# A two-layer decoder kernel: forget and query projections turned to features on partitions, chunk sums by scans, values turned after their product, another order of the last tiles

## What is computed

```python
forget = lb + (1 - lb) * sigmoid(f)          # lb: one lower bound per feature
q, k, log_f = silu(q), 1 - forget, log(forget)
b = cumsum(log_f)                            # inside each chunk of 32 tokens
q_dec = q * exp(b)
k_inv = k * exp(-b)
k_tail = k * exp(b_last - b)
scores = tril(q_dec @ k_inv.T)
o = scores @ v + q_dec @ state
state = state * exp(b_last) + k_tail.T @ v
```

## Time and profile before

| | |
|---|---|
| median of 3 runs | 1162.54 us (1162.41 to 1162.78) |
| profiled execution | 1162.58 us, span 1160.5 us |
| TensorE matmul busy | 1133.5 us (98%) |
| VectorE busy | 895.1 us (77%) |
| ScalarE busy | 752.8 us (65%) |
| GpSimd busy | 131.5 us (11%) |
| granted TensorE clock, mean | 0.998 |

### The profile page before, as it was taken

The page is one execution under the profiler, slowest core; times in us unless marked ns, Lnnn a source line. Parts: engine busy times, 40 slices in busy tenths (PEclk is TensorE's granted clock), DMA queues, the critical chain, the costliest instruction groups (busy, mean ns, idle before and its releaser), DMA issues.

```text
span 1160.5 us, 17159 instructions
## 1 busy us (share of the span) xinstructions
PE 1133.5 (98%) x5862; PEld 900.0 (78%) x5862; DVE 895.1 (77%) x1233; ACT 752.8 (65%) x960; POOL 131.5 (11%) x91
## 2 busy tenths in 40 slices
PE   9999999999999999999999999999999999999996
PEld 7778777776888888888788875776888888888775
DVE  6542468637999999999885359836999999999886
ACT  7563122445887888778665449645878888788665
POOL 0000000001221212211000000001212122121000
PEclk9999999999999999999999999999999999999999
DMA  9662222523999999999761220322899999999731
GB/s 368 250 234 73 73 74 73 177 96 122 336 377 380 379 388 371 382 374 380 277 276 68 95 73 2 146 105 96 323 361 378 391 374 384 376 372 390 267 137 73
DMA packets 50596, 286.30 MB, mean 247 GB/s; under 512 B 9321, under 2 KB 9597, under 8 KB 21358
## 3 DMA queue, kind: packets, MB, share of 16 engines
q1 hardware_dynamic: 37086, 250.93, 56.5%
q0 software_dynamic: 13456, 34.65, 8.1%
HBM read 271.38 MB, written 30.41 MB: 260 GB/s over the span
## 4 chain that ended last, share of the span: by engine, by line
PE 86%; DVE 6%; ACT 3%; DMA 3%; issue 1%; SPq 0%; ACTq 0%; POOLq 0%; DVEq 0%
PE psum L568 80%; PE psum L974 2%; DVE arena L2689 2%; ACT whi L1416 2%; DMA arena<-vscr,cur 1%; DVE arena L2702 1%; PE psum L1015 1%; DMA arena<-yscr 1%; DVE wlo L1987 1%; DMA raw<-w_dense_dram 1%; PE psum L885 1%; ACT ahi L1416 1%; DVE wlo L1991 0%; ACT arena L1416 0%; DVE h L2522 0%
## 5 line engine op out<-in xcount | busy, mean ns | idle before, releaser
L1987 DVE TENSOR_TENSOR wlo<-raw,whi 128x2048 fp32r<-128x2048 f32 x200 | 456.1, 2289 | 70.6 <-ACT whi L1416 57.4
L568 PE MATMUL psum<-whi,ahi 128*128 128x512 f32 (+1 forms) x1184 | 468.0, 397 | 4.8 <-ACT ahi L1416 4.4
L568 PE MATMUL psum<-wlo,ahi 128*128 128x512 f32 (+1 forms) x1184 | 456.6, 387 | 0.9 <-DVE wlo L1991 0.9
L568 PE MATMUL psum<-whi,alo 128*128 128x512 f32 (+1 forms) x1184 | 451.9, 387 | 0.0
L1416 ACT ACTIVATE whi<-raw 128x2048 fp32r<-128x2048 f32 x200 | 382.8, 1916 | 44.5 <-PE psum L568 44.5
L568 PEld LDWEIGHTS psum<-whi,ahi 128*128 128x128 f32 x1184 | 222.5, 188 | 53.8 <-issue 6.8
L568 PEld LDWEIGHTS psum<-whi,alo 128*128 128x128 f32 x1184 | 222.3, 188 | 46.3
L568 PEld LDWEIGHTS psum<-wlo,ahi 128*128 128x128 f32 x1184 | 222.6, 188 | 42.8 <-DVE wlo L1991 1.3
L1416 ACT ACTIVATE arena<-psum 128x512 f32<-128x512 f32 (+3 forms) x150 | 83.2, 564 | 114.6 <-PE psum L568 90.6
L1416 ACT ACTIVATE ahi<-psum 128x512 fp32r<-128x512 f32 x146 | 82.0, 592 | 86.6 <-PE psum L974 39.3
L2797 POOL DMA_INDIRECT arena<-vscr,cur x32 | 69.5, 2171 | 386.0 <-DVE cur L2408 370.8
(11 more groups left out here) (221 smaller groups left out, 893.8 us busy)
## 6 DMA issues: line engine op xcount, KB each, us to landing
raw<-w_moe_dram SPq DMA_DIRECT2D x192, 1024.0 KB, 8.8
raw<-w_dense_dram SPq DMA_DIRECT2D x34, 1024.0 KB, 9.0
yscr<-arena POOLq DMA_DIRECT2D x2, 4096.0 KB, 23.1
arena<-yscr SPq DMA_DIRECT2D x6, 1024.0 KB, 7.3
vscr<-arena POOLq DMA_DIRECT2D x8, 512.0 KB, 2.9
h<-x_dram SPq DMA_DIRECT2D x4, 512.0 KB, 7.8
arena<-w_proj_dram POOLq DMA_DIRECT2D x2, 1024.0 KB, 7.7
arena<-yscr SPq DMA_DIRECT2D x4, 512.0 KB, 4.5
```

The lines of the kernel that those rows point to most:

```text
L568: return nc.tensor.matmul(o, l, r, start=start, stop=stop, **kw)
L1987: tt(wlo[:, b % SPL, :], raw[:, b % RAW, :], halves(whi[:, b % SPL, :]), ALU.subtract).then_inc(lo_ready, 1)
```

## The change

- The blocks' order is v, f, q, g. v keeps the form "act"; f and q are made with weights stationary, so that bank hh is head hh with time along columns.
- The lower bound is one number per partition; VectorE scales the sigmoid in one pass (multiply and add by per-partition numbers). `lower` goes.
- The chunk sum is VectorE's `tensor_tensor_scan` per head: state = keep * state + log f, with keep 0 at each chunk's first token; then b_last - b by a subtraction. `cum` goes, with its constant matrices; the exponentials read SBUF.
- Inverse keys and decayed queries come out in the form that the score products need; `kq_T` goes. The tail keys now have to be turned: `tail_T`, four transposes behind each of the first four tiles of g, copied out by ScalarE.
- The values of the attention are made like the keys (24 products of 512 columns), multiplied by the tokens' norm (VectorE), turned by four transposes behind aq1's first tile, and get their bias as they leave PSUM.
- The last `dense` goes through its tiles in the order `ENDS`; ScalarE and VectorE finish token block 2 ahead of the last gate.

The diff, cut to what the prediction speaks of:

```diff
-BLK = {"f": 0, "q": 1, "v": 2, "g": 3, "C": 4, "H": 5, "B": 6, "out0": 7, "ple0": 9,
+BLK = {"v": 0, "f": 1, "q": 2, "g": 3, "C": 4, "H": 5, "B": 6, "out0": 7, "ple0": 9,
...
+ENDS = [(0, 0), (0, 1), (1, 0), (0, 2), (1, 1), (1, 2), (0, 3), (1, 3)]
...
-        READ = {1: (g_sig, 0), 2: (g_silu, 0), 3: (g_v, 0), 8: (s_add, 0), 10: (M[0]["gt"], 0),
+        READ = {1: (g_v, 0), 2: (g_sig, 0), 3: (g_silu, 0), 8: (s_add, 0), 10: (M[0]["gt"], 0),
...
-                    sp.wait_ge(M[1]["gt"], 8 + tb)
+                    sp.wait_ge(M[1]["sg"], TB + tb)
...
-                    pe.wait_ge(*((t_z, 5) if q == 0 else (t_v, q)))
+                    pe.wait_ge(*((t_z, 5), (t_v, 1), (t_z, 3), (t_v, 2))[q])
...
-            def lower(i, q):
...
-                for hh in range(HEADS):
-                    last = mm(PS[4][:, hh * P:(hh + 1) * P], area(AR_ONE32, P), diag[:, hh, :],
-                              True, True)
-                last.then_inc(g_cum, 1)
...
-            dense(BLK["f"], "act", before=wait_first, mid=later_T, after=lower, order=TILES[1:],
+            dense(BLK["v"], "act", before=wait_first, mid=later_T, order=TILES[1:],
...
-            def cum(tb):
-                pe.wait_ge(g_log, tb + 2)
+            def tail_T(tb):
...
-                mm(PS[4][:, :], hc("triI"), F[:, tb, :], True, True)
-                mm(PS[5][:, :], hc("triS"), F[:, tb, :], True, True)
+                    pe.wait_ge(g_ktail, HEADS)
...
-                    at = (tb * HEADS + hh) * CPB
-                    last = mm(PS[6][:, at:at + CPB], F[:, tb, hh * P:(hh + 1) * P], hc("ind"),
-                              True, True)
-                last.then_inc(g_cum, 1)
-            def kq_T(tb):
...
-                for bank, at in ((7, AR_F), (6, AR_Q)):
-                    for hh in range(HEADS):
-                        last = nc.tensor.transpose(PS[bank][:, hh * P:(hh + 1) * P],
-                                                   area(at, TB, 512)[:, tb, hh * P:(hh + 1) * P],
-                                                   ident)
-                    last.then_inc(g_kqT, 1)
-            dense(BLK["q"], "act", after=lambda i, q: cum(q) if i == 1 else None)
-            dense(BLK["v"], "act", after=lambda i, q: kq_T(q) if i == 1 else None)
+                    last = nc.tensor.transpose(PS[4 + tb][:, hh * P:(hh + 1) * P],
+                                               area(AR_F, HEADS, SEQ)[:, hh, tb * P:(tb + 1) * P],
+                                               ident)
+                last.then_inc(g_kqT, 1)
+            dense(BLK["f"], "w")
+            dense(BLK["q"], "w")
...
+                pe.wait_ge(g_KT, tb + 1)
...
-                    pe.wait_ge(g_KT, TB)
-                    pe.wait_ge(g_QT, TB)
+                    pe.wait_ge(g_kinv, HEADS)
+                    pe.wait_ge(g_qdec, HEADS)
+                cols = slice(tb * P, (tb + 1) * P)
...
-                    last = mm(PS[4 + tb][:, hh * P:(hh + 1) * P], KT_[:, tb, hh * P:(hh + 1) * P],
-                              QT_[:, tb, hh * P:(hh + 1) * P], True, True)
+                    last = mm(PS[4 + tb][:, hh * P:(hh + 1) * P], KT_[:, hh, cols],
+                              QT_[:, hh, cols], True, True)
...
-            dense(BLK["g"], "act", after=lambda i, q: scores(q) if i == 1 else None)
+            dense(BLK["g"], "act", after=lambda i, q: scores(q) if i == 1 else tail_T(q))
...
-                          QT_[:, tb, hh * P + c * CHUNK:hh * P + (c + 1) * CHUNK],
+                          QT_[:, hh, n * CHUNK:(n + 1) * CHUNK],
...
-                    pe.wait_ge(g_ktail, TB)
+                    pe.wait_ge(g_KT, TB)
...
                 else:
-                    dense(k + 1, "act")
+                    dense(k + 1, "act", order=ENDS)
...
-            for q in range(4):
+            for q in range(2):
...
-                            t_ = slice(tb * P, (tb + 1) * P)
-                            mm(o, ahi[:, kt, t_], whi[:, s, w], kt == 0, False)
-                            mm(o, ahi[:, kt, t_], wlo[:, s, w], False, False)
-                            last = mm(o, alo[:, kt, t_], whi[:, s, w], False, kt == KT - 1)
...
+                o = PS[q][:, :]
+                for kt in range(KT):
+                    w = slice(kt * 256 + q * P, kt * 256 + (q + 1) * P)
+                    mm(o, whi[:, s, w], ahi[:, kt, :], kt == 0, False)
+                    mm(o, whi[:, s, w], alo[:, kt, :], False, False)
+                    last = mm(o, wlo[:, s, w], ahi[:, kt, :], False, kt == KT - 1)
+                if q == 0:
+                    last.then_inc(d_done, 3)
+                else:
+                    last.then_inc(w_used, 1)
+            def value_T():
+                pe.wait_ge(t_v, 1)
+                pe.wait_ge(t_z, 4)
+                for t in range(TB):
+                    last = nc.tensor.transpose(PS[3][:, t * P:(t + 1) * P],
+                                               area(AR_VT1, SEQ)[:, t * P:(t + 1) * P], ident)
+                last.then_inc(t_pT, 1)
...
+                if i == 0 and q == 0:
+                    value_T()
                 if i == 0 and 0 < q < 3:
...
             nc.scalar.activation(e3, e3, ACT.Exp).then_inc(g_log, 1)
...
+            B = area(AR_G, HEADS, SEQ)
             splits(4)
-            for tb in range(TB):
-                group_done(act, BLK["f"], tb)
-                nc.scalar.activation(F[:, tb, :], PS[tb][:, :], ACT.Sigmoid).then_inc(g_sig, 1)
-            splits(5)
-            for tb in range(TB):
-                act.wait_ge(g_k, tb + 3)
-                nc.scalar.activation(F[:, tb, :], F[:, tb, :], ACT.Ln).then_inc(g_log, 1)
-            dec = area(AR_DEC, 64)
-            def query(tb):
-                group_done(act, BLK["q"], tb)
-                nc.scalar.activation(Q[:, tb, :], PS[tb][:, :], ACT.Silu).then_inc(g_silu, 1)
-            for tb in range(TB):
...
-                nc.scalar.activation(E[:, tb, :], PS[4][:, :], ACT.Exp).then_inc(g_eb, 1)
-                nc.scalar.activation(et, PS[4][:, :], ACT.Exp, scale=-1.0).then_inc(g_enb, 1)
...
-                nc.scalar.activation(yt, PS[5][:, :], ACT.Exp).then_inc(g_esf, 1)
...
-            splits(8)
             act.wait_ge(n_t, 2 * TB + 1)
...
                 copy(V[:, tb, :], PS[tb][:, :]).then_inc(g_v, 1)
-                act.wait_ge(g_kqT, 2 * tb + 2)
-                copy(Q[:, tb, :], PS[6][:, :]).then_inc(g_QT, 1)
+            splits(6)
+            for hh in range(HEADS):
+                group_done(act, BLK["f"], hh)
+                nc.scalar.activation(F[:, hh, :], PS[hh][:, :], ACT.Sigmoid).then_inc(g_sig, 1)
+            for hh in range(HEADS):
+                act.wait_ge(g_k, hh + 2)
+                nc.scalar.activation(F[:, hh, :], F[:, hh, :], ACT.Ln).then_inc(g_log, 1)
+            splits(7)
+            for hh in range(HEADS):
+                act.wait_ge(g_cum, hh + 1)
+                nc.scalar.activation(F[:, hh, :], F[:, hh, :], ACT.Exp).then_inc(g_esf, 1)
+                nc.scalar.activation(E[:, hh, :], B[:, hh, :], ACT.Exp).then_inc(g_eb, 1)
+                nc.scalar.activation(B[:, hh, :], B[:, hh, :], ACT.Exp, scale=-1.0).then_inc(g_enb, 1)
+            splits(8)
+            for hh in range(HEADS):
+                group_done(act, BLK["q"], hh)
+                nc.scalar.activation(Q[:, hh, :], PS[hh][:, :], ACT.Silu).then_inc(g_silu, 1)
+            splits(9)
+            act.wait_ge(g_kinv, HEADS)
+            for tb in range(TB):
+                act.wait_ge(g_kqT, tb + 1)
+                copy(K[:, tb, :], PS[4 + tb][:, :]).then_inc(g_KT, 1)
             splits(10)
...
-                    act.wait_ge(g_qdec, TB)
+                    act.wait_ge(g_sc, TB)
...
                         half_means(6)
-                    if q == 1:
                         half_square(6, 0, 1)
+                    if q == 2:
                         halves_sqrt(6, 0)
                         last_sqrt(1)
+                        half_square(6, 2, 1)
+                        halves_sqrt(6, 2)
+                        last_half(1)
+                        last_half(2)
                 link(nc.scalar.activation(ssb[:, 0, 0:1], ssb[:, 0, 0:1], ACT.Sqrt))
-                last_half(1)
-                half_square(6, 2, 1)
-                halves_sqrt(6, 2)
                 last_sqrt(3)
-                last_half(2)
                 last_half(3)
...
-            e3, lb, lb2 = area(AR_LBL, 3, HEADS), area(AR_LBL + 12, HEADS), area(AR_LB, 2, AW)
+            e3, lb, above = area(AR_LBL, 3, HEADS), area(AR_LBL + 12, HEADS), area(AR_LBL + 16, HEADS)
...
+            link(ts(above, lb, -1.0, 1.0, ALU.mult, ALU.add))
+            dve.wait_ge(s_consts, 16)
+            keep = area(AR_KEEP, SEQ)
+            link(nc.vector.tensor_copy(area(AR_KEEP, TB, P),
+                                       hc("reset").unsqueeze(1).to_broadcast([P, TB, P])))
...
+            def chunks(x, hh):
```

(70 more changed lines are left out.)

97 lines of the change are left out of this document (22 added, 75 removed).

## The result

The changed kernel takes 1143.60 us (median of four executions, 1143.25 to 1144.23) beside 1162.66 for the kernel before in the same comparison: ratio 0.983, 95% interval 0.9816 to 0.9843. The forecast was 1144.5, a gain of 18.0; by the medians 19.1 were gained (their quotient is 0.9836, inside the interval). The interval of the ratio stands for a gain of 18.3 to 21.4 us, so the forecast gain lies just under it. The profiled execution took 1143.25, span 1141.4, against 1162.58 and 1160.5 before.

What follows compares the result with a forecast made beforehand. TensorE, busy 98% of the span, was taken to bound the kernel; gains of 13.0 (projections), 4.8 (values) and 0.2 (end) sum to 18.0 off 1162.58, forecasting 1144.5 us with unrounded terms, range 1142.9 to 1148.0.

Steps and rivals of the forecast that it cites:

- Part 1: Projections on TensorE: constant-matrix sums, k and q transposes and lower-bound spreading go, tail-key transposes come; 13.0 us gained.
- Part 2: Attention values on TensorE: 24 products of 512 columns and four transposes replace 96 products of 128 columns; 4.8 us gained.
- rival B: Attention score loop: its start is set by something other than the projection in front, losing 4.8 us: 1149.3; chance 5%.
- Part 3: Last tiles and row passes: new tile order finishes three token blocks early, but a table load takes its place; 0.2 us gained.
- The side work: ScalarE and VectorE work beside the projections and attention is ready before TensorE asks for it; cost 0.
- TensorE waits for all four tail keys: Behind g's first tile, at 81.8 on the old clock, TensorE needs the tail keys, forecast ready at 71.8.
- the ten on record: Slack at the tail keys: they end at 71.8, ten microseconds ahead of TensorE's need at 81.8.
- Rival A: First-stage scans cost far more than 0.68 us, so TensorE waits for tail keys; slower above 7.7 us per scan; chance 2%.
- the far bound: Scan priced at the longest vector instruction, 2.29 us: tail keys end at 77.1, 4.7 ahead of need.
- Rival C: Tail's two table switches cost up to a further 1.28 us load each: 1145.8 or 1147.1; chance 5%.
- Zero writes: Two 4 MB POOL writes zeroing the expert result move behind the last Ln, from 43.3 to 61.5; cost 0.

Runs made afterwards that it cites:

- the run of this part alone: Kernel before with only the projections' lines of the change (f and q with weights stationary, scans, turned tail keys): 1150.75 us beside 1164.33, ratio 0.9882.
- the end alone: Kernel before with only the new order of the last eight tiles and the matching ScalarE, VectorE and SyncE lists: 1163.47 us beside 1164.33, ratio 0.9992.
- the three kernels with the old end: Kernel before, and it with only the projections' change (ratio 0.9882) or only the values' change (0.9973): 9.9 us from last product to span's end.
- the run with two queues: Changed kernel with two scalings of finished rows moved behind the last gate's sigmoid and the last first half's output issued by ScalarE: 1142.85 us, ratio 0.9821.
- the fourfold kernel: Changed kernel with each of the four scans run four times over: 1157.13 us, 11.6 over the changed kernel on this chip.
- both scalings behind the gate: Changed kernel with ScalarE's two scalings of finished first halves moved behind the last gate's sigmoid: 1144.47 us beside 1145.56 for the changed kernel.

## Why the prediction was right in kind and small in size

The gain came where it was forecast and by the mechanisms forecast, but two sizes were wrong. The step that failed is the end's term: 0.2 us, worked out only as far as the last row pass, where 0.8 was measured. Besides, everything between the convolutions and the attention was put at nothing, where 0.5 was measured.

- **Part 1, -13.0.** Measured 12.94 by the convolutions' first product, 13.15 with the later start taken out, and 13.12 in the same way in the run of this part alone. The price of an insertion as the period of the tiles less 2.72 held for the sum. Of the four kinds only the one that was added can be seen by itself: the tail keys' transposes start at 82.01, 85.21, 88.42 and 91.62, a period of 3.20, so 0.49 each as forecast.
- **The 0.5 us behind it** was no term of the sum. I had costed the stretch from the convolutions to the attention as unchanged; part 1 takes a wait of 0.4 us with it, by 0.3 us on ScalarE ahead of one split. Why stays open, and so does the remaining 0.2.
- **Part 2, -4.8.** Measured 4.85 alone and 4.9 in the whole. The chain of the score loop moved with its input, as argued against rival B.
- **Part 3, -0.2.** The mis-sized term: measured 0.8, in the changed kernel twice and in the end alone, against the three kernels with the old end. The chain I worked out was good to 0.1: row pass 0.26 earlier, load done at 1133.97 and sigmoid at 1134.67, which with the 18.3 of the other parts are the 1152.3 and 1153.0 on record. But I ended the working at the row pass and took the 3.2 us from the last output issue to the end, and the issue behind the pass, from the earlier trace rows as fixed. They are not: last row pass start to the end is 4.45 before (1160.5 - 1156.05) and 3.92 after. Before, the row passes of two token blocks start 0.9 us apart and SyncE issues their four outputs back to back, from 1155.97 to 1157.31; after, the last block's two stand alone, 1138.26 and 1138.63. Only 0.1 of the 0.5 lies in the issues (the last starts 0.51 behind the end of the row pass, then 0.40); 0.4 lies behind the last issue (3.21 us to the end of the span, then 2.81). In the run with two queues, where the last two are issued together, it is 3.17 again. That outputs issued this close hold each other up fits all of this, but no run varies it alone; that the 0.5 us go with the new end is shown.
- **The side work, cost 0.** Right, but the cover was not where I put it. Tail keys were ready at 72.9 (71.8 on record), wanted at 82.0; the scan took 1.22, inside the bounds, where the working used 0.68. The Trainium skill (DVE: opcode table, instruction layouts, handler registers and perf-mode slots, section Datapath and trigger behaviour) says that the built-in scan runs at half throughput; this trace agrees, with 1.22 against 0.68 for a pass that reads the same. What was wrong here, at no cost in time, is "TensorE waits for all four tail keys" as the first wait: every bank that a group leaves is also awaited, and the one that q's first group leaves is emptied by ScalarE behind the exponentials. Its slack is 2.9, under a third of the ten on record. Rival A's wait starts where a scan takes some 2.6 us (1.22 and 1.25 more are just covered), not 3.2, and costs four per scan as said, plus the clock behind the stall. So at the far bound, a scan of 2.29, the cover would have been about 1 us (an estimate, 4 x 0.26) and not the 4.7 on record. The forecast would have been the same, but that it held there was luck: this wait was on no list.
- **Rival C**, a dearer switch: taken away, the switch gave back 1.24. From the end of the work before the load to the sigmoid behind it stand 1.31 us. The Trainium skill (ScalarE: Activation LUTs, section What ACT_TABLE_LOAD costs) counts 2.66 us; the trace goes against it in this place, where the row of 1.28 was nearly the whole price.
- **Zero writes, cost 0:** 0 in both places.
- **Sum:** 18.0 against 19.1 by the spans: 0.6 of the miss lies in the end, 0.5 behind the convolutions, and the two large terms are right to 0.1 or 0.2.

## What to carry to other kernels

Work the tail out to the landing of the last byte: what leaves the last engine later than the last pass, and what queues with it, is part of the term. For cover (the time by which side work is ready before the bound engine asks for it), list every wait of that engine in order (operands and also the buffers that it overwrites) and take the smallest slack; a run that repeats one hidden instruction two, three and four times measures it to a few tenths. And ahead of a table load on the path do only what must be ahead: finished work can go behind it.

## What the runs showed of the hardware

- A scan of 128x512 takes 1.22 to 1.23 us, 1.8 times a pass that reads the same (0.68), and repeated ones start some 1.26 apart (four of them take 5.00 in the fourfold kernel).
- A stall has a second price. Behind the waits of 9.7 and 4.7 us TensorE went on at half clock (granted 0.50 and 0.52, the 1.2 GHz level) and lost 2.3 and 1.6 us more.
- The same shows without a new wait: with both scalings behind the gate, TensorE was busy 1.20 of 3.40 us ahead of the output projection, much as in the other kernels (1.53 of 3.50 in the changed one), but in that execution the clock then fell, and all behind it stood 1.6 us later than by the landmarks ahead (0.52 behind the changed kernel, then 2.12). Such a stretch of 3.4 us stands in some profiled executions and not in others. It fits the spread of the times: of the kernel before on the first of the three chips, the one execution with a mean granted clock of 0.998 took 1162.5 us and the fifteen with 0.996 took 1163.6 to 1165.3, but these were not profiled. Busy times by stretch of the kernel with both scalings behind the gate:

```profile
194.60:198.00 3.40, 1.20 (x10) 0.98 (x9) 2.70 (x3) 1.02 (x2) 0.00 (x0) 1.00 0.16 19
198.00:201.40 3.40, 3.40 (x11) 2.61 (x11) 3.30 (x7) 3.40 (x6) 0.00 (x0) 0.60 0.72 294
```
